# Padding so that the large on-chip tensors of a transformer kernel begin at multiples of 512 bytes

## The chip, the core and the metric

The kernel is one program on one NeuronCore of a Trainium2 chip. The engines that matter here are TensorE (PE in the profile, its weight loads PEld), VectorE (DVE), ScalarE (ACT), GpSimd (POOL) and the queue of SyncE (SP), which issues all DMAs. They share the state buffer (SBUF), in which every tensor occupies the same byte range of each of 128 partitions, and TensorE writes to eight PSUM banks. The metric is the device time of one execution in microseconds (us); lower is better. Times are compared on fresh runs of both kernels.

## The reference

One block of a conformer-like layer and two blocks of a hybrid layer over 256 tokens of width 1024, all float32. Cut to what costs time:

```python
x = x + 0.5 * swiglu_ffn(rms_norm(x), ffn1_w13, ffn1_w2)      # 1024 -> 2*2816 -> 1024
proj = rms_norm(x) @ w_in                                      # 1024 -> 2568: convolution + attention
x = x + y @ w_out
x = x + 0.5 * swiglu_ffn(rms_norm(x), ffn2_w13, ffn2_w2)
h = rms_norm(x)
h = h + gdn_mixer(rms_norm_2(h), gdn_w_in, ...)                # 1024 -> 4112, gated delta rule, -> 1024
h = h + swiglu(rms_norm_2(h), ffn_w_in[0], ffn_w_out[0])
h = h + (p[0] @ ple_w_proj[0]) * sigmoid(rms_norm_2(h) @ ple_w_gate[0])
k, v = shared_kv(h, w_kv)                                      # stick-breaking attention
h = h + sb_mixer(rms_norm_2(h), k, v, w_q, w_out)
h = h + swiglu(...); h = h + (p[1] @ ple_w_proj[1]) * sigmoid(...)
```

There are thus four feed-forward blocks, each with a product 1024 -> 5632 ("up") and one 2816 -> 1024 ("down"), three mixers and two gates.

## The kernel before

**Products.** Every large product is made from pieces of the TensorE format fp32r. A float32 number is kept as a high part and a low part, and one product of 128 rows, 128 tokens and up to 512 columns takes three matmuls (`passes`, lines 1527 to 1529):

```python
pe.matmul(psum, lhs[0], rhs[0], start=start, stop=False, ...)   # L1527
pe.matmul(psum, lhs[0], rhs[1], start=False, stop=False, ...)   # L1528
return pe.matmul(psum, lhs[1], rhs[0], start=False, stop=stop, ...)  # L1529
```

The first operand, `lhs`, is the stationary one: it is loaded into the array ahead of the matmul. The second, `rhs`, moves through the array. The profile writes `bank<-moving,stationary`, so `bank<-whi,xThi 128x512` is a matmul with 512 moving columns of the weight buffer `whi` and a stationary piece of `xThi`. Numbers in names are left out there: `xThi` also stands for `xThi2`, `xTlo` for `xTlo2`, `u` for `u4`, `y` for `y4`.

**Where the operands lie.** The weights come from memory through four ring buffers of 8192 bytes, `raw0` to `raw3` (DMA). ScalarE rounds a slot into `whi0` to `whi3` (L390), VectorE takes the rest into `wlo0` to `wlo3` (L1018). The turned activations are the other operand, one of four pairs:

- `xThi`, `xTlo`: the normalised input of the up products, the mixers, the gates and the mixers' outputs. 2976 matmuls of 128x512 have them stationary. In 864 matmuls of 128x256 (`block_cols`) they move and a piece of `whi` or `wlo` is stationary.
- `hThi`, `hTlo`: the hidden state of a feed-forward block, stationary in its down product: 22 k-tiles x 2 token tiles x 2 halves x 3 = 264 matmuls of 128x512 a block, 1056 in all.
- `xThi2`, `xTlo2`: a second normalised input, stationary in two products of the stick-breaking mixer (`block_rows(s + 4, xT2, ...)` and `s + 6`), 96 matmuls of 128x512.
- `pThi`, `pTlo`: the per-layer embedding, stationary in `ple_product`, 48 matmuls of 128x512.

The remaining matmuls are narrower: transposes by `ident`, attention scores, the delta rule. They read float32 operands that are not split.

**Allocation.** `sb(name, shape)` takes the next free bytes of every partition, rounded up to 32. `region(always, *turns)` lays several sets of tensors over the same room: the feed-forward set, the first mixer's, the second mixer's and the third mixer's all begin where the permanent tensors end. The first free byte is 1152. The permanent tensors are, in order, `raw`, `whi`, `wlo`, `X`, `xs`, `xThi`, `xTlo`, `gain`, `ident`, `ones`, `upto`, then many small tensors up to `head_gain`, then the shared room. From the declared sizes the places in a partition are, in bytes:

| tensor | start before | rest by 512 | start after | rest by 512 |
|---|---|---|---|---|
| raw0 (raw1 to wlo3 follow every 8192) | 1152 | 128 | 1536 | 0 |
| X, xs | 99456, 107648 | 128 | 99840, 108032 | 0 |
| xThi, xTlo | 115840, 124032 | 128 | 116224, 124416 | 0 |
| ident | 140416 | 128 | 140800 | 0 |
| narrow_m | 146240 | 320 | 146624 | 192 |
| shared room, hThi, qkT, vs | 149472 | 480 | 150016 | 0 |
| hTlo | 172000 | 480 | 172544 | 0 |
| xThi2, xTlo2 | 165856, 174048 | 480 | 166400, 174592 | 0 |
| pThi, pTlo | 204768, 206816 | 480 | 205312, 207360 | 0 |
| AT (delta rule) | 191584 | 96 | 190976 | 0 |
| u, y (first mixer) | 149472, 158144 | 480, 448 | 218112, 154112 | 0 |
| u4, y4 (second mixer) | 215584, 219744 | 32, 96 | 221696, 213504 | 0 |
| last byte used | 227936 | | 228480 | |

A stationary piece of the four pairs is 512 bytes a partition and begins a multiple of 512 bytes behind its tensor's start; a moving piece of `whi` or `wlo` is 2048 bytes and begins a multiple of 2048 (512 in `block_cols`, where it is stationary) behind it. So the rests of the table hold for every piece.

**Order of the work.** All five engines run instruction lists that are written out by hand, with semaphores between them. SP issues a weight slot when VectorE has finished the slot four earlier; ScalarE and VectorE split slots ahead of TensorE.

Of the kernel before, what the change touches and what calls it, by code (L numbers as in the profile page):

```python
# [6 lines left out]
F32 = mybir.dt.float32  # L7
F32R = mybir.dt.float32r
# [4 lines left out]
P = 128  # L13
# [4 lines left out]
def build_program(nc, a, out):  # L18
# [6 lines left out]
    SEQ, D = a["x"].shape[1:]  # L25
    NT = SEQ // P
# [3 lines left out]
    DC = a["conv_b"].shape[1]  # L30
    CT = DC // P
    TAPS = a["conv_w"].shape[1]
    PAD = TAPS - 1
    H1 = a["forget_b"].shape[1]
    D1 = DC // H1
    H2 = a["gdn_a_log_2"].shape[1]
    HG = H2 // 4
    W4 = a["gdn_conv_2"].shape[1]
    PAD4 = W4 - 1
# [74 lines left out]
    with ExitStack() as ctx:  # L114
        def sb(name, shape, dt=F32):
            return ctx.enter_context(nc.sbuf_tensor(name, shape, dt))
# [20 lines left out]
            return sem(engine), names.index(name) + 1  # L137

        bank = [ctx.enter_context(nc.psum_tensor(f"bank{i}", [P, 512], F32)) for i in range(8)]
        raw = [sb(f"raw{i}", [P, SLOT]) for i in range(RAW)]  # L140
        whi = [sb(f"whi{i}", [P, SLOT], F32R) for i in range(SPLIT)]
        wlo = [sb(f"wlo{i}", [P, SLOT], F32R) for i in range(SPLIT)]
# [28 lines left out]
        dt_bias = sb("dt_bias", [P, H2])  # L171
        head_gain = sb("head_gain", [P, 3, P])
        GDNG, KG, QG = range(3)

        def region(always, *turns):
            got = []
            with ExitStack() as phase:
                got += [phase.enter_context(nc.sbuf_tensor(n, s, d)) for n, s, d in always]
                for specs in turns:
                    with ExitStack() as turn:  # L180
                        got += [turn.enter_context(nc.sbuf_tensor(n, s, d)) for n, s, d in specs]
            return got
# [6 lines left out]
             ("pp", [P, NT, D], F32), ("gate_s", [P, NT, D], F32)],  # L189
            [("row_chan", [CT, P], F32), ("row_tap", [TAPS, DC], F32), ("row_tap4", [W4, QKV * P], F32)])  # L190

        (u, gs, y, a_nat, ln_row, qz, kz, v1, mask1, mask_r, ident_r, diag, zf, zfe, lf, cumx, p2, pT1, nmx, rsum, rinv, yA,
         yst, yms, yrs, y_nat, flT, c_sums, c_nmean, c_ssq, c_var, c_rstd) = region([
            ("u", [P, CT, PAD + SEQ], F32), ("gs", [P, CT, SEQ], F32), ("y", [P, CT, SEQ], F32),
            ("a_nat", [P, NT, DC], F32), ("ln_row", [P, 3, DC], F32),
            ("qz", [P, H1, SEQ], F32), ("kz", [P, H1, SEQ], F32), ("v1", [P, NT, DC], F32),
            ("mask1", [P, P], F32), ("mask_r", [P, P], F32R), ("ident_r", [P, P], F32R), ("diag", [P, CT * PE_TAPS, P], F32),
            ("zf", [P, NT, H1], F32), ("zfe", [P, NT, H1], F32),
            ("lf", [P, NT, H1], F32), ("cumx", [P, NT, H1 // 2, D1 + 1], F32),
            ("p2", [P, 2, 384], F32), ("pT1", [P, 2, 384], F32), ("nmx", [P, H1, NT], F32),  # L200
            ("rsum", [P, NT, H1], F32), ("rinv", [P, NT, H1], F32), ("yA", [P, NT, DC], F32),
            ("yst", [P, NT], F32), ("yms", [P, NT], F32), ("yrs", [P, NT], F32),
            ("y_nat", [P, NT, DC], F32), ("flT", [2 * H1, SEQ], F32), ("c_sums", [P, NT], F32), ("c_nmean", [P, NT], F32),
            ("c_ssq", [P, 2, NT], F32), ("c_var", [P, 2, NT], F32), ("c_rstd", [P, 2, NT], F32)])
        LNG, LNB, ONG = range(3)
        aff = xs[:, :, DC:]


        (qkT, sg, zab, eab, gl, lkq, vec, knat, bv, dg, dec, AT, QKT, pair, lvl, maskT, gident_r, gmask_r, S, oss, oms, ors, v_or_TU, u4, y4,
         sq4) = region(  # L210
            [("qkT", [P, 2 * H2, SEQ], F32), ("sg", [P, NT, D], F32), ("zab", [P, NT, 2 * H2], F32),
             ("eab", [P, NT, 2 * H2], F32), ("gl", [P, NT, 2 * H2], F32), ("lkq", [P, NT, 2 * H2], F32),
             ("vec", [P, 10, NT, H2], F32), ("knat", [P, H2, P], F32), ("bv", [P, NT, D], F32),
             ("dg", [P, 4, P], F32), ("dec", [P, 4, P], F32), ("AT", [P, HG, 4, P], F32),
             ("QKT", [P, HG, 4, P], F32), ("pair", [P, P], F32), ("lvl", [P, 5, 64], F32), ("maskT", [P, P], F32), ("gident_r", [P, P], F32R), ("gmask_r", [P, P], F32R), ("S", [P, H2, P], F32),
             ("oss", [P, NT, H2], F32), ("oms", [P, NT, H2], F32), ("ors", [P, NT, H2], F32),
             ("v_or_TU", [P, H2 * SEQ], F32), ("u4", [P, 4, PAD4 + SEQ], F32), ("y4", [P, 4, SEQ], F32),
             ("sq4", [P, 4, SEQ], F32)])
        abT = dg[0:4 * H2, 0:2, :].rearrange("p a b -> p (a b)")
        vT = v_or_TU[:].rearrange("p (h t) -> p h t", h=H2)  # L220

# [1960 lines left out]
```

## Time and profile before

| | |
|---|---|
| median of 3 runs | 1281.78 us (1281.6 to 1283.31) |
| the profiled execution | 1281.92 us, span of its trace 1280.2 us |
| TensorE | busy 1264.0 us of the span |
| DVE, ACT, POOL | busy 759.9, 621.4, 75.5 us |
| granted clock | 0.996 of full, on average |

"Busy" for TensorE counts a matmul from its start to a modelled end, and matmuls overlap in the array. What a matmul costs in a dense row of them is the distance from its start to the next one's start, which the timeline shows; the text calls it the step.

### The profile page before, as it was taken

To read this page: it belongs to the slowest core of one execution; us is meant where nothing else is said; L and a number is where in the kernel's file an instruction comes from. 1 tells how busy PE (TensorE), PEld (TensorE's weight loads), DVE (VectorE), ACT (ScalarE), POOL (GpSimd) and SP (SyncE) were. 2 spreads that over 40 slices of the span, in tenths; PEclk is the share of its full clock that TensorE was granted. 3 is DMA by queue.
4 is the path that set the end of the run, shared out by engine and by line. 5 is a ranking of instruction groups with operands and counts; after the bars stand their busy time and mean duration, and the time that the engine had idled before them with its cause. 6 is when DMAs were issued, how large, how long until landed. Compare 5 with 4: busy or idle time off the path is not lost.

```text
span 1280.2 us, 16498 instructions
## 1 busy us (share of the span) xinstructions
PE 1264.0 (99%) x6711; PEld 1077.9 (84%) x6711; DVE 759.9 (59%) x891; ACT 621.4 (49%) x798; POOL 75.5 (6%) x125
## 2 busy tenths in 40 slices
PE   8999999999999999999999999999999999999998
PEld 6888888988888888899999888888887888888887
DVE  4655436896654545777776655554677636545435
ACT  5544426665544433655613544443466745444433
POOL 1000002002000000400001000000023000000000
PEclk9999999999999999999998999999999999999999
DMA  8965555452566564545102476555365427665530
GB/s 271 286 182 186 192 186 151 171 172 72 172 194 190 174 227 136 194 133 188 60 1 67 122 243 194 190 177 186 135 219 174 159 59 239 190 200 180 196 132 33
DMA packets 140427, 212.27 MB, mean 166 GB/s; under 512 B 10265, under 2 KB 101277, under 8 KB 140348
## 3 DMA queue, kind: packets, MB, share of 16 engines
q1 hardware_dynamic: 140352, 211.22, 50.7%
q8 instruction: 53, 0.87, 0.3%
q14 instruction: 22, 0.18, 0.0%
HBM read 210.14 MB, written 1.05 MB: 165 GB/s over the span
## 4 chain that ended last, share of the span: by engine, by line
PE 91%; DVE 3%; ACT 3%; POOL 1%; issue 1%; DMA 1%; SPq 0%; ACTq 0%; DVEq 0%; POOLq 0%
PE bank L1527 27%; PE bank L1529 26%; PE bank L1528 26%; PE bank L1936 2%; PE bank L1666 2%; PE bank L1556 1%; PE bank L1947 1%; PE bank L1955 1%; DVE y L1126 1%; DVE wlo L1018 1%; ACT whi L390 1%; PE bank L1907 1%; PE bank L1900 1%; PE bank L1861 1%; DMA X<-in_x_dram 1%
## 5 line engine op out<-in xcount | busy, mean ns | idle before, releaser
L1018 DVE TENSOR_TENSOR wlo<-raw,whi 128x2048 fp32r<-128x2048 f32 (+1 forms) x190 | 416.4, 2196 | 289.0 <-ACT whi L390 288.8
L390 ACT ACTIVATE whi<-raw 128x2048 fp32r<-128x2048 f32 x190 | 363.1, 1915 | 237.8 <-PE bank L1529 228.6
L1527 PE MATMUL bank<-whi,xThi 128*128 128x512 f32 x1024 | 405.2, 396 | 3.1 <-DVE xTlo L1041 1.0
L1529 PE MATMUL bank<-whi,xTlo 128*128 128x512 f32 x1024 | 399.5, 390 | 0.0
L1528 PE MATMUL bank<-wlo,xThi 128*128 128x512 f32 x1024 | 398.9, 390 | 0.0
L1527 PEld LDWEIGHTS bank<-whi,xThi 128*128 128x128 f32 x1024 | 192.3, 188 | 43.2 <-issue 2.0
L1529 PEld LDWEIGHTS bank<-whi,xTlo 128*128 128x128 f32 x1024 | 192.2, 188 | 41.2
L1528 PEld LDWEIGHTS bank<-wlo,xThi 128*128 128x128 f32 x1024 | 192.5, 188 | 38.2
L1527 PE MATMUL bank<-whi,hThi 128*128 128x512 f32 x352 | 140.5, 399 | 0.0
L1529 PE MATMUL bank<-whi,hTlo 128*128 128x512 f32 x352 | 139.5, 396 | 0.0
L1528 PE MATMUL bank<-wlo,hThi 128*128 128x512 f32 x352 | 139.5, 396 | 0.0
L473 ACT ACTIVATE silu<-bank 128x256 f32<-128x256 f32 x88 | 33.6, 383 | 122.0 <-PE bank L1529 122.0
L1527 PE MATMUL bank<-xThi,whi 128*128 128x256 f32 x288 | 82.7, 287 | 0.0
L1528 PE MATMUL bank<-xTlo,whi 128*128 128x256 f32 x288 | 82.2, 286 | 0.0
L1529 PE MATMUL bank<-xThi,wlo 128*128 128x256 f32 x288 | 82.2, 285 | 0.0
L1529 PEld LDWEIGHTS bank<-whi,hTlo 128*128 128x128 f32 x352 | 66.3, 188 | 16.2
L1528 PEld LDWEIGHTS bank<-wlo,hThi 128*128 128x128 f32 x352 | 66.3, 188 | 15.6
L1527 PEld LDWEIGHTS bank<-whi,hThi 128*128 128x128 f32 x352 | 66.3, 188 | 15.6
L916 POOL TENSOR_SCALAR meansq<-sumsq 128x1 f32<-128x1 f32 x16 | 12.5, 781 | 882.8 <-ACT xs L414 699.5
L1092 DVE TENSOR_TENSOR hnat<-silu,bank 128x256 f32<-128x256 f32 x88 | 36.7, 417 | 46.7 <-ACT silu L473 46.7
L1527 PEld LDWEIGHTS bank<-xThi,whi 128*128 128x128 f32 x288 | 55.9, 194 | 0.1
L1529 PEld LDWEIGHTS bank<-xThi,wlo 128*128 128x128 f32 x288 | 56.0, 194 | 0.0
(394 smaller groups left out, 1198.3 us busy)
## 6 DMA issues: line engine op xcount, KB each, us to landing
raw<-in_ffn_w_dram SPq DMA_DIRECT2D x176, 256.0 KB, 4.1
raw<-in_ffn_w_in_dram SPq DMA_DIRECT2D x176, 256.0 KB, 3.9
raw<-in_ffn_w_dram SPq DMA_DIRECT2D x22, 1024.0 KB, 5.0
raw<-in_ffn_w_out_dram SPq DMA_DIRECT2D x22, 1024.0 KB, 5.0
raw<-in_gdn_w_in_dram SPq DMA_DIRECT2D x16, 1024.0 KB, 5.5
raw<-in_w_in_dram SPq DMA_DIRECT2D x10, 1024.0 KB, 5.1
raw<-in_ple_w_gate_dram SPq DMA_DIRECT2D x8, 1024.0 KB, 4.9
raw<-in_w_kv_dram SPq DMA_DIRECT2D x8, 1024.0 KB, 6.1
```

Source lines behind the costliest of these rows:

```text
L390: act.activation(whi[w % SPLIT][:], raw[w % RAW][:], ACT.Copy).then_inc(w_hi, 1)
L473: act.activation(silu[:, j % 2, t, :], bank[2 * (j % 2) + t][:, 0:256], ACT.Silu).then_inc(sem("ffn_silu"), 1)
L1018: dve.tensor_tensor(wlo[w % SPLIT][:, c], raw[w % RAW][:, c], whi[w % SPLIT][:, c].bitcast(F32), ALU.subtract).then_inc(w_lo, 1)
L1092: dve.tensor_tensor(hnat[:, j % 2, t, :], silu[:, j % 2, t, :], bank[2 * (j % 2) + t][:, 256:512], ALU.mult).then_inc(sem("ffn_h"), 1)
L1126: ins = dve.scalar_tensor_tensor(out=y[:, c, :], in0=src, scalar=tap[:, c, k:k + 1], in1=y[:, c, :], op0=ALU.mult, op1=ALU.add)
L1527: pe.matmul(psum, lhs[0], rhs[0], start=start, stop=False, skip_group_check=True)
L1528: pe.matmul(psum, lhs[0], rhs[1], start=False, stop=False, skip_group_check=True)
L1529: return pe.matmul(psum, lhs[1], rhs[0], start=False, stop=stop, skip_group_check=True)
L1556: ins = pe.transpose(bank[4 + b][:, k * P:(k + 1) * P], xs[:, t, (4 * b + k) * P:(4 * b + k + 1) * P], ident[:])
L1666: ins = pe.transpose(bank[4 + j % 2][:, k * SEQ + t * P:k * SEQ + (t + 1) * P], hnat[:, j % 2, t, k * P:(k + 1) * P], ident[:])
L1861: ins = pe.matmul(bank[6][:, col:col + 1], sq4[:, c, t * P:(t + 1) * P], ones[:, 0:1], start=True, stop=True)
L1936: ins = pe.matmul(bank[q][:, h * c.stop:(h + 1) * c.stop], A_[q][k, h, :], T[q][k, h, c], start=True, stop=True)
```

## The change

Two unused tensors are added, `front` (96 floats, 384 bytes) ahead of `raw0` and `level` (40 floats, 160 bytes) ahead of the shared room. The lists of the first and second mixer's tensors are put in another order: those whose size is a multiple of 512 bytes come first, the others (`u`, `cumx`, `u4`, `lvl`, `vec` and the small ones) last. Nothing else changes. On each of the five engines the built program has the same instructions in the same order with the same waits as before; only addresses differ, so no rows of the order are shown.

```diff
@@ build_program
         bank = [ctx.enter_context(nc.psum_tensor(f"bank{i}", [P, 512], F32)) for i in range(8)]
+        sb("front", [P, 96])
         raw = [sb(f"raw{i}", [P, SLOT]) for i in range(RAW)]
         whi = [sb(f"whi{i}", [P, SLOT], F32R) for i in range(SPLIT)]
...
         head_gain = sb("head_gain", [P, 3, P])
         GDNG, KG, QG = range(3)
+        sb("level", [P, 40])
 
         def region(always, *turns):
...
-            ("u", [P, CT, PAD + SEQ], F32), ("gs", [P, CT, SEQ], F32), ("y", [P, CT, SEQ], F32),
+            ("gs", [P, CT, SEQ], F32), ("y", [P, CT, SEQ], F32),
...
-            ("zf", [P, NT, H1], F32), ("zfe", [P, NT, H1], F32),
-            ("lf", [P, NT, H1], F32), ("cumx", [P, NT, H1 // 2, D1 + 1], F32),
...
+            ("y_nat", [P, NT, DC], F32), ("flT", [2 * H1, SEQ], F32),
+            ("u", [P, CT, PAD + SEQ], F32), ("cumx", [P, NT, H1 // 2, D1 + 1], F32),
...
-            [("qkT", [P, 2 * H2, SEQ], F32), ("sg", [P, NT, D], F32), ("zab", [P, NT, 2 * H2], F32),
+            [("qkT", [P, 2 * H2, SEQ], F32), ("sg", [P, NT, D], F32), ("knat", [P, H2, P], F32), ("bv", [P, NT, D], F32),
...
+             ("u4", [P, 4, PAD4 + SEQ], F32), ("lvl", [P, 5, 64], F32), ("vec", [P, 10, NT, H2], F32),
```

## Rows read from the trace of the kernel before

**Rows 1.** The page: busy time of each engine, share of the span, instructions.

```profile
span 1280.2 us, 16498 instructions
PE 1264.0 (99%) x6711; PEld 1077.9 (84%) x6711; DVE 759.9 (59%) x891; ACT 621.4 (49%) x798; POOL 75.5 (6%) x125
```

**Rows 2.** The page: the chain of work that ended last, by engine.

```profile
PE 91%; DVE 3%; ACT 3%; POOL 1%; issue 1%; DMA 1%; SPq 0%; ACTq 0%; DVEq 0%; POOLq 0%
```

**Rows 3.** Timeline of TensorE, stationary xT, up product: start us, us, instruction.

```profile
99.55 0.39 PE L1528 MATMUL bank<-wlo,xThi 128*128 128x512 f32 x1
...
104.54 0.39 PE L1529 MATMUL bank<-whi,xTlo 128*128 128x512 f32 x1
```

**Rows 4.** Timeline of TensorE, stationary hT, down product of the first block.

```profile
180.18 0.40 PE L1529 MATMUL bank<-whi,hTlo 128*128 128x512 f32 x1
180.42 0.39 PE L1527 MATMUL bank<-whi,hThi 128*128 128x512 f32 x1
...
186.74 0.40 PE L1527 MATMUL bank<-whi,hThi 128*128 128x512 f32 x1
```

**Rows 5.** Timeline of TensorE, stationary xThi2 and xTlo2, third mixer.

```profile
976.56 0.40 PE L1529 MATMUL bank<-whi,xTlo 128*128 128x512 f32 x1
...
981.48 0.40 PE L1529 MATMUL bank<-whi,xTlo 128*128 128x512 f32 x1
```

**Rows 6.** Timeline of TensorE, stationary pT, the whole first token tile.

```profile
822.37 0.39 PE L1528 MATMUL bank<-wlo,pThi 128*128 128x512 f32 x1
...
824.70 0.39 PE L1529 MATMUL bank<-whi,pTlo 128*128 128x512 f32 x1
```

**Rows 7.** Timeline of TensorE after a transpose, last gate product, stationary xT.

```profile
1262.04 0.39 PE L1528 MATMUL bank<-wlo,xThi 128*128 128x512 f32 x1
...
1263.89 0.39 PE L1527 MATMUL bank<-whi,xThi 128*128 128x512 f32 x1
...
1266.84 0.39 PE L1528 MATMUL bank<-wlo,xThi 128*128 128x512 f32 x1
```

**Rows 8.** Windows of the down product and of two windows with the lower clock.

```profile
core 0: us, PE busy (x) PEld busy (x) DVE busy (x) ACT busy (x) POOL busy (x), PEclk, DMA share, GB/s
553.00:560.00 7.00, 7.00 (x48) 7.00 (x47) 7.00 (x14) 2.69 (x3) 0.00 (x0) 0.76 0.47 151
670.00:690.00 20.00, 20.00 (x164) 19.75 (x164) 14.34 (x26) 5.96 (x24) 1.21 (x2) 0.83 0.35 106
150.00:198.00 48.00, 48.00 (x207) 38.59 (x206) 19.47 (x12) 16.03 (x12) 0.87 (x2) 1.00 0.49 165
```

**Rows 9.** Timeline of TensorE, 128x256, moving xT, stationary whi or wlo.

```profile
560.05 0.28 PE L1527 MATMUL bank<-xThi,whi 128*128 128x256 f32 x1
...
562.45 0.28 PE L1529 MATMUL bank<-xThi,wlo 128*128 128x256 f32 x1
```

**Rows 10.** Timeline of TensorE, 128x256, with 16 and 8 stationary columns.

```profile
214.91 0.28 PE L1641 MATMUL bank<-xThi,narrow_m 128*16 128x256 f32 x1
...
216.76 0.28 PE L1527 MATMUL bank<-xThi,whi 128*128 128x256 f32 x1
```

**Rows 11.** Timeline of TensorE in the delta rule: unsplit float32, merged over x8.

```profile
635.62 1.06 PE L1936 MATMUL bank<-core_hi,AT 128*128 128x128 f32 x8
636.52 1.06 PE L1936 MATMUL bank<-core_hi,xs 128*128 128x128 f32 x8
```

**Rows 12.** Groups of VectorE: the convolutions' taps.

```profile
L1126 DVE SCALAR_TENSOR_TENSOR y<-u,tap,y 128x256 f32<-128x256 f32 x96 | 39.2, 475 | 0.0
L1283 DVE SCALAR_TENSOR_TENSOR y<-u,tap,y 128x256 f32<-128x256 f32 x72 | 29.1, 480 | 0.0
```

**Rows 13.** The chain that ended last: its DMA (start us, us).

```profile
4.34 6.75 DMA X<-in_x_dram
```

**Rows 14.** The page: the DMA queue, packets, MB, share of 16 engines.

```profile
q1 hardware_dynamic: 140352, 211.22, 50.7%
```

More of the change, by code:

```diff
@@ L190, in build_program @@
             [("row_chan", [CT, P], F32), ("row_tap", [TAPS, DC], F32), ("row_tap4", [W4, QKV * P], F32)])
-        (u, gs, y, a_nat, ln_row, qz, kz, v1, mask1, mask_r, ident_r, diag, zf, zfe, lf, cumx, p2, pT1, nmx, rsum, rinv, yA,
-         yst, yms, yrs, y_nat, flT, c_sums, c_nmean, c_ssq, c_var, c_rstd) = region([
-            ("u", [P, CT, PAD + SEQ], F32), ("gs", [P, CT, SEQ], F32), ("y", [P, CT, SEQ], F32),
+        (gs, y, a_nat, ln_row, qz, kz, v1, mask1, mask_r, ident_r, diag, p2, pT1, yA, y_nat, flT, u, cumx, zf, zfe, lf,
+         nmx, rsum, rinv, yst, yms, yrs, c_sums, c_nmean, c_ssq, c_var, c_rstd) = region([
+            ("gs", [P, CT, SEQ], F32), ("y", [P, CT, SEQ], F32),
             ("a_nat", [P, NT, DC], F32), ("ln_row", [P, 3, DC], F32),
@@ L197, in build_program @@
             ("mask1", [P, P], F32), ("mask_r", [P, P], F32R), ("ident_r", [P, P], F32R), ("diag", [P, CT * PE_TAPS, P], F32),
-            ("zf", [P, NT, H1], F32), ("zfe", [P, NT, H1], F32),
-            ("lf", [P, NT, H1], F32), ("cumx", [P, NT, H1 // 2, D1 + 1], F32),
-            ("p2", [P, 2, 384], F32), ("pT1", [P, 2, 384], F32), ("nmx", [P, H1, NT], F32),
-            ("rsum", [P, NT, H1], F32), ("rinv", [P, NT, H1], F32), ("yA", [P, NT, DC], F32),
-            ("yst", [P, NT], F32), ("yms", [P, NT], F32), ("yrs", [P, NT], F32),
@@ L203, in build_program @@
-            ("y_nat", [P, NT, DC], F32), ("flT", [2 * H1, SEQ], F32), ("c_sums", [P, NT], F32), ("c_nmean", [P, NT], F32),
-            ("c_ssq", [P, 2, NT], F32), ("c_var", [P, 2, NT], F32), ("c_rstd", [P, 2, NT], F32)])
+            ("p2", [P, 2, 384], F32), ("pT1", [P, 2, 384], F32), ("yA", [P, NT, DC], F32),
+            ("y_nat", [P, NT, DC], F32), ("flT", [2 * H1, SEQ], F32),
+            ("u", [P, CT, PAD + SEQ], F32), ("cumx", [P, NT, H1 // 2, D1 + 1], F32),
+            ("zf", [P, NT, H1], F32), ("zfe", [P, NT, H1], F32), ("lf", [P, NT, H1], F32), ("nmx", [P, H1, NT], F32),
@@ L205, in build_program @@
+            ("rsum", [P, NT, H1], F32), ("rinv", [P, NT, H1], F32),
+            ("yst", [P, NT], F32), ("yms", [P, NT], F32), ("yrs", [P, NT], F32), ("c_sums", [P, NT], F32),
+            ("c_nmean", [P, NT], F32), ("c_ssq", [P, 2, NT], F32), ("c_var", [P, 2, NT], F32), ("c_rstd", [P, 2, NT], F32)])
         LNG, LNB, ONG = range(3)
         aff = xs[:, :, DC:]
-        (qkT, sg, zab, eab, gl, lkq, vec, knat, bv, dg, dec, AT, QKT, pair, lvl, maskT, gident_r, gmask_r, S, oss, oms, ors, v_or_TU, u4, y4,
-         sq4) = region(
-            [("qkT", [P, 2 * H2, SEQ], F32), ("sg", [P, NT, D], F32), ("zab", [P, NT, 2 * H2], F32),
-             ("eab", [P, NT, 2 * H2], F32), ("gl", [P, NT, 2 * H2], F32), ("lkq", [P, NT, 2 * H2], F32),
-             ("vec", [P, 10, NT, H2], F32), ("knat", [P, H2, P], F32), ("bv", [P, NT, D], F32),
-             ("dg", [P, 4, P], F32), ("dec", [P, 4, P], F32), ("AT", [P, HG, 4, P], F32),
[L215 to L218, printed above, removed]
@@ new lines, in build_program @@
+        (qkT, sg, knat, bv, dg, dec, AT, QKT, pair, maskT, gident_r, gmask_r, S, v_or_TU, y4, sq4, u4, lvl, vec,
+         zab, eab, gl, lkq, oss, oms, ors) = region(
+            [("qkT", [P, 2 * H2, SEQ], F32), ("sg", [P, NT, D], F32), ("knat", [P, H2, P], F32), ("bv", [P, NT, D], F32),
+             ("dg", [P, 4, P], F32), ("dec", [P, 4, P], F32), ("AT", [P, HG, 4, P], F32),
+             ("QKT", [P, HG, 4, P], F32), ("pair", [P, P], F32), ("maskT", [P, P], F32),
+             ("gident_r", [P, P], F32R), ("gmask_r", [P, P], F32R), ("S", [P, H2, P], F32),
+             ("v_or_TU", [P, H2 * SEQ], F32), ("y4", [P, 4, SEQ], F32), ("sq4", [P, 4, SEQ], F32),
+             ("u4", [P, 4, PAD4 + SEQ], F32), ("lvl", [P, 5, 64], F32), ("vec", [P, 10, NT, H2], F32),
+             ("zab", [P, NT, 2 * H2], F32), ("eab", [P, NT, 2 * H2], F32), ("gl", [P, NT, 2 * H2], F32),
+             ("lkq", [P, NT, 2 * H2], F32), ("oss", [P, NT, H2], F32), ("oms", [P, NT, H2], F32),
+             ("ors", [P, NT, H2], F32)])
```

## Prediction

> **What bounds the kernel now.** I read the page first: TensorE is busy for 1264.0 of 1280.2 us [rows 1], and the chain of work that ended last is 91% TensorE [rows 2]. Busy time counts overlapping matmuls, so I went on to the timeline and measured the step, from one start to the next, in stretches where no record is missing. That is the price of a matmul here, and it is what an address could change.
>
> With a piece of xT stationary, 22 steps from 99.55 to 104.54 us take 4.99 us: 226.8 ns each [rows 3]. With a piece of hT stationary, 28 steps from 180.18 to 186.74 take 6.56 us: 234.3 ns each [rows 4]. The work is the same: 128x512, moving `whi` or `wlo`, full clock (1.00 in this stretch) [rows 8]. The two stages differ in their order (a down product alternates between two banks), so the step could belong to the stage. The third mixer says otherwise: its `block_rows` runs in the up products' manner, but with `xThi2` and `xTlo2`, and 21 steps take 4.92 us: 234.3 ns [rows 5]. With pT, 10 steps take 2.33 us, 233 ns [rows 6]. And the last gate product, in the down products' manner but with xT, runs at 231.3 ns for 8 steps after a transpose and then settles: 13 steps in 2.95 us, 226.9 ns [rows 7]. So the longer step goes with the tensor that is stationary. By the table of places xT begins at rest 128 by 512, a whole number of 64 bytes; hT, xT2 and pT begin at 480, which is 32 past one.
>
> **What the change does, step by step.** No instruction, wait or queue entry is added, removed or moved; nothing is queued behind anything new.
>
> 1. Stationary pieces of hT and xT2 go from rest 480 to rest 0. I expect them to run as xT does: 234.3 - 226.8 = 7.5 ns less a step. 1056 + 96 = 1152 matmuls x 7.5 ns = 8.6 us. They lie on the path: in the stretch of the down product TensorE has no idle time in 48 us, while DVE works 19.47 us, ACT 16.03 us and the DMA engines 49% [rows 8]. A stretch shorter by 3% leaves those covers more than double what is needed, so nothing becomes late behind it.
> 2. pT: its short stretches look like the unsettled steps of xT, 233 against 231.3 ns [rows 6, 7]. 48 x 1.7 ns = 0.1 us.
> 3. xT as stationary (2976 matmuls) and the 128x256 ones (864, step 2.40 us / 20 = 120 ns [rows 9]): operands go from rest 128 to rest 0, both by the same 384 bytes, so their distance stays. No row has an fp32r operand of 128 columns at rest 0. Bounds: a gain down to the step of the nearest row with a cheaper weight load, 16 steps in 1.85 us = 115.6 ns for 16 and 8 stationary columns [rows 10], 4.4 ns less; a loss up to the 7.5 ns of hT. I take 0, because 128 is already a whole number of 64 bytes, and because the row with the smaller step has fewer columns to load as its evident reason.
> 4. Unsplit float32 matmuls: with AT stationary (rest 96, also 32 past a multiple of 64) 8 take 0.90 us, with xs (rest 128) 0.89 us [rows 11]. Price 0: these matmuls do not feel the rest.
> 5. VectorE's taps: 475 ns with one set of rests, 480 with another [rows 12]. All 168 of them at 5 ns would be 0.8 us, but DVE is 3% of the chain [rows 2]; I take 0, at most 0.2 either way.
> 6. Transfers: their engines are at 50.7% [rows 14] and only the first load, 6.75 us of X, is on the chain [rows 13]. No row shows a transfer to rest 0. I take 0; bounds 0 and a gain of 0.5 us, as a small part of that one load.
>
> Sum: 8.6 + 0.1 = 8.7 us. Against the profiled execution, 1281.92 - 8.7 = 1273.2; the median is 0.14 us lower, so 1273.1 us.
>
> A rule of the Trainium skill speaks against the whole sum. The page "SBUF — State Buffer", section "Specifications (TRN2)", gives 16-byte lines and lets a new line cost only where it has fewer than two hits. By that rule every start here, a multiple of 32 before and after, is equally good and the sum would be 0. The steps of 226.8 and 234.3 ns don't contradict the rule outright, since it could be something other than the start that tells the tensors apart; that is the first rival.
>
> **The rivals.**
>
> - *No change (0.13).* The longer step comes from where hT, xT2 and pT lie in the partition, not from the rest: all of them begin above byte 149,000, xT below 133,000, and this stays so after the change. The trace cannot part the two, since everything slow is at 480 and everything high is slow. Against it: hT, xT2 and pT are spread over 59,000 bytes and show the same step. Time 1281.8 us, or within about 1 us of it if only small terms move. The line rule of the Trainium skill's page "SBUF — State Buffer" gives this time too. The case in which the faster down product meets a late split belongs here, but the slack of rows 8 leaves it little.
> - *More than expected (0.08).* A start at 512 also frees xT and the 128x256 matmuls of some of their cost over bare streaming (512 columns at 2.4 GHz are 213.3 ns, the step 226.8). At the lower bound of step 3, 4.4 ns on all 5040 fp32r matmuls (4176 of 512 columns, 864 of 256) is 22.2 us more: 1250.9 us. Half of it gives 1262. Against it: the 120 ns of rows 9 and the 226.8 of rows 3 lie the same 13.4 ns above streaming, which looks like a fixed cost of the format. The Trainium skill's "TensorE: Matmul & The Clock Gate", section "Back-to-back issue gap", gives N/2.4 + 2.5 ns; by that page, as an estimate, the step could fall to 215.8 ns. No row of an fp32r matmul here comes down to it.
> - *Slower (0.06).* Rest 0 behaves as rest 480 does and the settled step of xT is a property of rest 128. For it: that step is not always there, it is reached only after some eight steps of 231.3 ns [rows 7], so it depends on how two streams fall against each other. Then 2976 x 7.5 ns = 22.3 us are lost and nothing is won: 1304.1 us. It decides from 2.9 ns more on the step of xT, where the 8.7 us are eaten.
>
> **How the numbers follow.** My forecast has 0.73: 1273.1, own range 1270.5 to 1276. The lower clock adds to that range: 0.76 in a 7 us window is 1.7 us lost, 0.83 in 20 us is 3.4 us [rows 8], and one such fall more or less is 1.7 us. The likeliest case and most of the no-change case (1279.5 to 1284) make up the 8 in 10, so the range reaches from 1266, which takes in a small extra gain of xT, to 1282.5. A measurement of this kernel tells about 0.2% (2.6 us) from no change. Faster than that: 0.73 + 0.08 and a little of the no-change case, 0.82. Slower: 0.06. The same: 0.12.
>
> **What the profile of the changed kernel would show.** Right: in the timeline of the first down product the step falls to 226.8 ns and so does that of `xThi2`; the first down product's 264 matmuls end 2.0 us earlier; xT and 128x256 keep 226.8 and 120. Wrong by the first rival: 234.3 in both places. Wrong by the second: under 225 in the up product. Wrong by the third: 230 or more there. It is also wrong if steps fall but the time does not; then the wait ahead of a down product's slots would show DVE or ACT as the releaser. The weakest step is the first: that the rest by 64, rather than something else that the slow tensors share, sets their step.

## The result, and the profile after

The changed kernel takes 1274.02 us (median of 6 runs, 1272.34 to 1275.8); the kernel before, on the same chip, 1281.74 us (6 runs, 1281.6 to 1283.35). The ratio is 0.9932, with a 95% interval of 0.9922 to 0.9942: 8.7 us less, between 7.4 and 10.0 (the two medians are 7.7 us apart). The prediction was 1273.1 us, with 8.7 us of gain. One execution of the kernel before, among those of the first group of experiments, had a low clock throughout (1571.78 us, 0.748 of full) and is left out of the ratios.

The profiled execution took 1272.45 us. Its page gives the span and the engines' busy times (they answer to [rows 1]), the chain by engine [rows 2] and the DMA queue [rows 14]:

```profile
span 1270.7 us, 16498 instructions
PE 1254.4 (99%) x6711; PEld 1076.0 (85%) x6711; DVE 759.9 (60%) x891; ACT 621.0 (49%) x798; POOL 75.7 (6%) x125
...
PE 91%; ACT 3%; DVE 3%; POOL 1%; issue 1%; DMA 0%; SPq 0%; ACTq 0%; DVEq 0%; POOLq 0%
...
q1 hardware_dynamic: 140352, 211.22, 50.8%
```

TensorE's busy time fell by 9.6 us and the span by 9.5; the counts, the other engines and the transfers stayed as they were. So the time came out of TensorE's matmuls, without a new wait. A step below is the distance between two printed starts divided by the number of steps; the starts are rounded to 0.01 us, so that a step worked out in this way is good to some 0.4 ns. Where it came from is in its timeline. In the down product of the first block, with hT stationary (answers to [rows 4]):

```profile
181.57 0.39 PE L1530 MATMUL bank<-whi,hThi 128*128 128x512 f32 x1
181.79 0.39 PE L1531 MATMUL bank<-wlo,hThi 128*128 128x512 f32 x1
182.02 0.39 PE L1532 MATMUL bank<-whi,hTlo 128*128 128x512 f32 x1
...
187.69 0.39 PE L1530 MATMUL bank<-whi,hThi 128*128 128x512 f32 x1
```

From the first to the last start there are 27 steps in 6.12 us: 226.7 ns, where it was 234.3. In the up product, with xT stationary (answers to [rows 3]), and in the third mixer, with xT2 (answers to [rows 5]):

```profile
109.14 0.39 PE L1531 MATMUL bank<-wlo,xThi 128*128 128x512 f32 x1
...
113.90 0.39 PE L1531 MATMUL bank<-wlo,xThi 128*128 128x512 f32 x1
...
971.52 0.39 PE L1531 MATMUL bank<-wlo,xThi 128*128 128x512 f32 x1
...
976.06 0.39 PE L1530 MATMUL bank<-whi,xThi 128*128 128x512 f32 x1
```

21 steps in 4.76 us are 226.7 ns, unchanged; 20 steps in 4.54 us are 227.0 ns (226.7 by the trace's nanoseconds), where it was 234.3. The 128x256 matmuls (answers to [rows 9]) kept their 120 ns, 19 steps in 2.28 us:

```profile
555.57 0.28 PE L1530 MATMUL bank<-xThi,whi 128*128 128x256 f32 x1
...
557.85 0.28 PE L1531 MATMUL bank<-xTlo,whi 128*128 128x256 f32 x1
```

The two spans differ by 9.5 us, the medians by 7.7. Part of that is the clock. The windows that answer to the first two of [rows 8]:

```profile
core 0: us, PE busy (x) PEld busy (x) DVE busy (x) ACT busy (x) POOL busy (x), PEclk, DMA share, GB/s
553.00:560.00 7.00, 7.00 (x60) 7.00 (x59) 5.18 (x6) 3.92 (x3) 0.00 (x0) 1.00 0.33 83
670.00:690.00 20.00, 19.51 (x158) 18.85 (x158) 14.71 (x26) 7.59 (x26) 2.20 (x2) 0.83 0.35 107
```

The fall in the first window, 7.00 x 0.24 = 1.7 us of full clock in the execution before, did not come in this one, and the two in the second did (0.17 x 20 = 3.4 us in both). By the steps it cost a little less: 16 matmuls of 256 columns took some 213 ns instead of 120, which is 1.5 us. So of the 9.5 us between the spans some 1.5 us is the clock and 8.0 us is left for the steps.

### The profile page after: what moved, and what is told of

It reads as the page before. It is cut to its first block, busy times and chain, and to the rows that moved or that the text cites. A ratio compares the mean times of both kernels' runs of the same rounds, so it can differ in the third digit from the quotient of the medians.

```text
span 1270.7 us, 16498 instructions
## 1 busy us (share of the span) xinstructions
PE 1254.4 (99%) x6711; PEld 1076.0 (85%) x6711; DVE 759.9 (60%) x891; ACT 621.0 (49%) x798; POOL 75.7 (6%) x125
## 4 chain that ended last, share of the span: by engine, by line
PE 91%; ACT 3%; DVE 3%; POOL 1%; issue 1%; DMA 0%; SPq 0%; ACTq 0%; DVEq 0%; POOLq 0%
PE bank L1530 26%; PE bank L1532 26%; PE bank L1531 26%; PE bank L1939 2%; PE bank L1669 2%; PE bank L1559 1%; PE bank L1950 1%; DVE y L1129 1%; DVE wlo L1021 1%; PE bank L1958 1%; ACT whi L393 1%; PE bank L1910 1%; PE bank L1903 1%; PE bank L1864 1%; DMA raw<-in_ffn_w_dram 0%
## 5 line engine op out<-in xcount | busy, mean ns | idle before, releaser
L1531 PEld LDWEIGHTS bank<-xTlo,whi 128*128 128x128 f32 x288 | 55.2, 192 | 0.0
```

The source lines that it names most:

```text
L1531: pe.matmul(psum, lhs[0], rhs[1], start=False, stop=False, skip_group_check=True)
```

## The experiments

Theories are named by letters in the expectations. **A**, the prediction's: the stationary piece's own start decides, by 64 bytes. **B**: the place in the partition. **C**: the distance between the starts of the stationary and the moving piece, by 64 bytes. **D**: both must begin at a multiple of 512. **E**: the distance must be 0 by 512. **F**: the distance must be 0 by 256. B had fallen with the result itself: hT and xT2 still begin above byte 149,000, and their step is 226.7 ns.

"Distance" below is the start of the stationary piece less that of the moving one, by 256 bytes. In the kernel before, xT and the weights both begin at rest 128 (distance 0), and hT, xT2 and pT at 480: 480 - 128 = 352, which is 96 by 256. The kernels of a group ran on one chip with the kernel before, whose medians there were 1283.07, 1282.99 and 1283.51 us.

### First group: the stationary piece alone, or its partner

**room_only.** The kernel before, with 32 bytes ahead of the shared room: hT and xT2 begin at rest 0, the weights stay at 128.

```diff
         GDNG, KG, QG = range(3)
+        sb("level", [P, 8])
```

> The kernel before with one unused tensor of 32 bytes ahead of the shared room, nothing else: hT, xThi2 and pT go from rest 480 to rest 0 by 512, while the weight buffers and xT stay at rest 128. Theory A (the start of the stationary piece by 64 bytes sets the step of a 512-column matmul): all of the gain, step of hT 226.8 ns, about 1273 to 1274 us. Theory B (the place in the partition, not the rest): hT keeps 234.3 ns, 1281.8 us. Theory C (the distance between moving and stationary operand by 64 bytes): the distance is again a multiple of 64, so as A. Theory D (all large tensors must begin at a multiple of 512): no or only part of the gain, above 1277 us.

Measured: 1280.2 us, ratio 0.9979 (0.997 to 0.9988). The down product:

```profile
181.60 0.40 PE L1528 MATMUL bank<-whi,hThi 128*128 128x512 f32 x1
...
187.87 0.40 PE L1528 MATMUL bank<-whi,hThi 128*128 128x512 f32 x1
```

27 steps in 6.27 us: 232.2 ns, and in the third mixer 20 steps in 4.65 us, 232.5. With exactly the rest 0 that the prediction held to be the cause, three quarters of the longer step stayed. A falls; so does C, since the distance of 128 is a multiple of 64. The small gain fits its steps: 1152 x 2 ns = 2.3 us, and 2.7 us by the ratio.

**xt_32.** The changed kernel with only xT moved to rest 32 (`back` and the smaller `level` keep all that follows).

```diff
+        sb("shift", [P, 8])
         with ExitStack() as lent:
...
         xTlo = sb("xTlo", [P, KD, SEQ], F32R)
+        sb("back", [P, 8])
...
-        sb("level", [P, 40])
+        sb("level", [P, 24])
```

> The changed kernel with xThi and xTlo (and what shares their room) 32 bytes further, at rest 32 by 64; weights and the shared room stay at rest 0. A: the 2976 matmuls with xT stationary take 234.3 instead of 226.8 ns, 22.3 us more than the changed kernel, about 1296 us; the 864 matmuls of 256 columns, where xT moves, keep 120 ns. B: xT is low in the partition and keeps 226.8 ns, about 1274 us. C: as A for the 512-column ones, and the 256-column ones get slower too, by up to 7.5 ns each, 6.5 us more, about 1302 us.

Measured: 1287.02 us, ratio 1.0037 (1.0023 to 1.0051), slower than the kernel before. The up product, and the 128x256 matmuls of the second mixer:

```profile
101.59 0.40 PE L1533 MATMUL bank<-wlo,xThi 128*128 128x512 f32 x1
...
106.49 0.40 PE L1533 MATMUL bank<-wlo,xThi 128*128 128x512 f32 x1
...
560.49 0.28 PE L1532 MATMUL bank<-xThi,whi 128*128 128x256 f32 x1
...
562.70 0.28 PE L1533 MATMUL bank<-xTlo,whi 128*128 128x256 f32 x1
```

21 steps in 4.90 us: 233.3 ns with xT, while hT stayed at 227.0. The 128x256 matmuls went the other way, 19 steps in 2.21 us, 116.3 ns (116.8 as the mean of all settled ones). That was in no expectation. The sum in this run: over all steps whose records stand side by side, xT went from a mean of 227.4 to 233.0 ns, 2976 x 5.6 = 16.7 us where 22.3 was expected, and those of 256 columns from 120.6 to 117.6, 864 x 3.0 = 2.6 us back; 14.1 us net, and its span is 13.7 us longer than the changed kernel's, with the clock falling equally often in both.

**weights_32.** The changed kernel with the weight buffers at 32, xT at 64 and hT at 0: distances 32 and -32.

```diff
+        sb("shift", [P, 8])
         whi = [sb(f"whi{i}", [P, SLOT], F32R) for i in range(SPLIT)]
...
+        sb("back", [P, 8])
...
-        sb("level", [P, 40])
+        sb("level", [P, 24])
```

> The changed kernel with whi and wlo at rest 32 by 64, everything else at a multiple of 64. A: the 512-column matmuls, where the weights move, keep 226.8 ns; the 864 of 256 columns, where they are stationary, take up to 7.5 ns more, at most 6.5 us: 1274 to 1280 us. B: no change, about 1274 us. C: every product's distance is off by 32, so all 4176 matmuls of 512 columns take 234.3 ns: 31 us more, and up to 6.5 us for the narrow ones, 1305 to 1312 us.

Measured: 1294.28 us, ratio 1.0087 (1.0071 to 1.0103). xT and hT in the up and the down product:

```profile
101.88 0.40 PE L1533 MATMUL bank<-wlo,xThi 128*128 128x512 f32 x1
...
106.78 0.40 PE L1533 MATMUL bank<-wlo,xThi 128*128 128x512 f32 x1
...
181.72 0.40 PE L1533 MATMUL bank<-wlo,hThi 128*128 128x512 f32 x1
...
188.03 0.39 PE L1533 MATMUL bank<-wlo,hThi 128*128 128x512 f32 x1
```

233.3 and 233.7 ns (both 233.3 over all their settled steps). hT is at a multiple of 512 and xT at one of 64, and both have the longer step: the partner counts. The sign of a distance of 32 makes no difference.

**xt_and_weights_32.** Weights and xT both at 32, hT at 0: the same as weights_32 but that `back` stands behind `xTlo`.

```diff
+        sb("shift", [P, 8])
         whi = [sb(f"whi{i}", [P, SLOT], F32R) for i in range(SPLIT)]
...
         xTlo = sb("xTlo", [P, KD, SEQ], F32R)
+        sb("back", [P, 8])
...
-        sb("level", [P, 40])
+        sb("level", [P, 24])
```

> The changed kernel with both whi, wlo and xThi, xTlo at rest 32 by 64; the shared room stays at rest 0. A: xT slow as stationary (22.3 us) and the weights slow as stationary (up to 6.5 us): 1296 to 1303 us; hT stays at 226.8 ns. C: the distance of xT to the weights is a multiple of 64 again, so xT is fast, and hT, xThi2 and pT are off by 32 and slow: 1282 to 1283 us, as the kernel before. B: about 1274 us.

Measured: 1280.43 us, ratio 0.9983 (0.9974 to 0.9993).

```profile
101.60 0.39 PE L1533 MATMUL bank<-wlo,xThi 128*128 128x512 f32 x1
...
106.36 0.39 PE L1533 MATMUL bank<-wlo,xThi 128*128 128x512 f32 x1
...
181.62 0.40 PE L1532 MATMUL bank<-whi,hThi 128*128 128x512 f32 x1
...
187.93 0.39 PE L1532 MATMUL bank<-whi,hThi 128*128 128x512 f32 x1
```

xT at rest 32 runs at 226.7 ns here and ran at 233.3 in xt_32: the same start, another partner. hT at rest 0 has 233.7 ns (233.3 over all its settled steps). What is left is a rule of the two starts together.

### Second group: by how many bytes the distance counts

**all_128.** The kernel before with 160 bytes ahead of the shared room, and nothing else: weights, xT, hT, xT2 and pT all at rest 128; no `front`, no other order of the lists.

```diff
         GDNG, KG, QG = range(3)
+        sb("level", [P, 40])
```

> The kernel before with 160 unused bytes ahead of the shared room and nothing else: weights, xT, hT, xThi2 and pT all at rest 128 by 512. Theory E (formed after the first four runs: a 512-column matmul takes 226.8 ns only where the stationary piece and the moving piece begin at the same rest by 512; the rest itself is free): all of the gain, hT at 226.8 ns, 1272 to 1275 us. Theory D (the rest must be 0 by 512): hT stays above 232 ns, 1280 us as in the run with 32 bytes. Theory A (stationary rest by 64 alone) has already fallen for that run and would give the full gain too.

Measured: 1274.24 us (1272.58 to 1276.26), ratio 0.9932 (0.992 to 0.9945).

```profile
181.23 0.39 PE L1529 MATMUL bank<-wlo,hThi 128*128 128x512 f32 x1
...
187.57 0.39 PE L1530 MATMUL bank<-whi,hTlo 128*128 128x512 f32 x1
```

28 steps in 6.34 us: 226.4 ns, and 226.7 by the trace's nanoseconds. This one line has the whole gain of the change. D falls: nothing large begins at a multiple of 512.

**all_32.** The changed kernel with 32 bytes more in front: every large tensor at rest 32.

```diff
-        sb("front", [P, 96])
+        sb("front", [P, 104])
```

> [...] E: no change, 1272 to 1275 us, steps of 226.8 ns everywhere. A: all 4176 wide matmuls at 233 ns or more, 26 to 31 us more, above 1300 us. D: slower than the changed kernel, by an amount it does not say.

Measured: 1277.39 us, ratio 0.9956 (0.9943 to 0.997). The steps are the short ones, 27 in 6.12 us with hT, 226.7 ns:

```profile
181.52 0.39 PE L1531 MATMUL bank<-wlo,hThi 128*128 128x512 f32 x1
...
187.64 0.39 PE L1531 MATMUL bank<-wlo,hThi 128*128 128x512 f32 x1
```

So a stationary piece that is 32 past a multiple of 64 costs nothing, the plainest case against the prediction's step. The time is 3.4 us longer than the changed kernel's all the same. Two windows show part of why:

```profile
50.00:57.00 7.00, 7.00 (x25) 5.58 (x25) 2.89 (x2) 0.49 (x2) 0.00 (x0) 0.76 0.85 254
553.00:560.00 7.00, 7.00 (x48) 7.00 (x47) 6.49 (x12) 2.51 (x4) 0.00 (x0) 0.76 0.40 142
```

The granted clock fell in both, and in neither of them in the changed kernel; with the two between 670 and 690 us, which both executions have, this one had four falls against two. The profiled spans are 1275.6 and 1270.7 us. Of these 4.9 us the two additional falls are some 3.3 us: the steps with xT add up to 1.8 us more and those of the 256-column matmuls to 1.5. The other 1.6 us I can't place. Executions of the two kernels with the same mean clock of 0.994 differ by about as much, 1275.6 to 1276.0 against 1274.0 us of span, though on two chips.

**h256_x64.** The changed kernel with hT at 256 and xT2 at 64, weights at 0.

```diff
-            [("hThi", [P, KF, SEQ], F32R), ("hTlo", [P, KF, SEQ], F32R),
+            [("shift", [P, 64], F32), ("hThi", [P, KF, SEQ], F32R), ("hTlo", [P, KF, SEQ], F32R),
...
-            ("vs", [P, NT, D], F32), ("kn", [P, NT, D], F32), ("xThi2", [P, KD, SEQ], F32R), ("xTlo2", [P, KD, SEQ], F32R),
+            ("vs", [P, NT, D], F32), ("kn", [P, NT, D], F32), ("shift2", [P, 16], F32), ("xThi2", [P, KD, SEQ], F32R), ("xTlo2", [P, KD, SEQ], F32R),
```

> The changed kernel with hT and pT at rest 256 and xThi2, xTlo2 at rest 64; weights and xT at rest 0. It asks with which period the distance counts. E (512): hT above 231 ns, xT2 above 231 ns, 1280 to 1283 us. F (256): hT at 226.8 ns, 1273 to 1275 us, xT2 above 231 ns. C (64): both at 226.8 ns, 1272 to 1275 us, although the run with 32 bytes ahead of the room speaks against it.

Measured: 1275.78 us, ratio 0.9943 (0.993 to 0.9957). hT, and xT2:

```profile
181.62 0.39 PE L1530 MATMUL bank<-whi,hThi 128*128 128x512 f32 x1
...
187.74 0.39 PE L1530 MATMUL bank<-whi,hThi 128*128 128x512 f32 x1
...
974.97 0.39 PE L1531 MATMUL bank<-wlo,xThi 128*128 128x512 f32 x1
...
979.64 0.39 PE L1530 MATMUL bank<-whi,xThi 128*128 128x512 f32 x1
```

A distance of 256 is as good as none, 226.7 ns: E falls. A distance of 64 costs, 20 steps in 4.67 us, 233.5 ns (233.3 over all its settled steps): C falls again, and the longer step is nothing of odd 32-byte starts. F is left.

**h16_x384.** hT at 16 (its tensors made 16 bytes longer, the product reading from the fifth element on), xT2 at 384, with the changed kernel's other places.

```diff
-            [("hThi", [P, KF, SEQ], F32R), ("hTlo", [P, KF, SEQ], F32R),
+            [("hThi_", [P, 4 + KF * SEQ], F32R), ("even1", [P, 120], F32), ("hTlo_", [P, 4 + KF * SEQ], F32R), ("even2", [P, 120], F32),
...
+        hThi, hTlo = (x[:, 4:].rearrange("p (k t) -> p k t", k=KF) for x in (hThi_, hTlo_))
...
+            ("vs", [P, NT, D], F32), ("kn", [P, NT, D], F32), ("shift2", [P, 96], F32), ("xThi2", [P, KD, SEQ], F32R), ("xTlo2", [P, KD, SEQ], F32R),
```

> The changed kernel with hT at rest 16 and xThi2, xTlo2 at rest 384; pT, weights and xT at rest 0. E: a distance of 16 bytes is a distance, so hT goes above 231 ns and the time to 1280 to 1283 us; xT2 above 231 ns. If only distances of a whole SBUF line of 32 or 64 bytes count: hT keeps 226.8 ns and the time stays at 1273 to 1275 us.

The expectation's "line of 32 or 64 bytes" is a supposition; no run shows a line of either size. Measured: 1277.98 us, ratio 0.996 (0.9946 to 0.9973). xT2: 232.5 ns, as room_only's distance of 128, which 384 is by 256. hT gave something new. The same product in the first block, and in the third:

```profile
181.24 0.39 PE L1533 MATMUL bank<-whi,hTlo_ 128*128 128x512 f32 x1
...
187.59 0.39 PE L1531 MATMUL bank<-whi,hThi_ 128*128 128x512 f32 x1
...
869.70 0.39 PE L1532 MATMUL bank<-wlo,hThi_ 128*128 128x512 f32 x1
...
875.77 0.40 PE L1531 MATMUL bank<-whi,hThi_ 128*128 128x512 f32 x1
```

28 steps in 6.35 us are 226.8 ns; 26 steps in 6.07 us are 233.5. Transposes cut each of the four down products into three rows of hT matmuls: 24, 228 and 12. In the first, second and fourth product the 24 ran long (233.4 ns), the 228 short (226.7) and the 12 long; in the third the 24 and the 228 ran long (855 to 908 us) and the 12 short. Each of the twelve rows keeps one pace to its end. Its first step, from its first matmul to its second, was 312 or 313 ns ahead of the four short rows and 314 to 319 ns ahead of the eight long ones. So at a distance of 16 both paces are possible, and a row keeps the one it has fallen into.

### Third group: the other distances, one operand of two, and a version for both widths

The first three were one execution each, so their times have no interval; their steps are what counts.

**h128_x192** and **h96_x160** are h256_x64 with other sizes of `shift` and `shift2`: 32 and 48 floats, 24 and 40 floats.

> The changed kernel with hT and pT at rest 128 and xThi2, xTlo2 at rest 192; weights and xT at rest 0. Theory F (the distance of the two operands counts by 256): hT as at distance 384, 232.3 to 232.5 ns; xT2 at 192 above 230 ns. One look, about 1280 us. If the sign of the distance mattered and the period were 512, hT could have any step from 226.7 to 235.

> The changed kernel with hT and pT at rest 96 and xThi2, xTlo2 at rest 160; weights and xT at rest 0. F: 96 is the same as the 352 of the kernel before by 256, so hT shows 234.3 ns, and about 1282 us; xT2 at 160 above 230 ns. Period 512 would leave hT free to differ from 234.3.

Measured: 1279.98 us, hT 27 steps in 6.27 us, 232.2 ns, xT2 21 steps in 4.81 us, 229.0 ns, less than the 230 that was expected at least; and 1282.95 us. The rows are those of xT2 in h128_x192 and of hT in h96_x160:

```profile
977.33 0.39 PE L1530 MATMUL bank<-whi,xThi 128*128 128x512 f32 x1
...
982.14 0.39 PE L1530 MATMUL bank<-whi,xThi 128*128 128x512 f32 x1
...
181.51 0.39 PE L1530 MATMUL bank<-whi,hThi 128*128 128x512 f32 x1
...
188.07 0.39 PE L1531 MATMUL bank<-wlo,hThi 128*128 128x512 f32 x1
```

28 steps in 6.56 us, 234.3 ns for hT in h96_x160, and 233.5 ns for its xT2. h96_x160 has the distance of the kernel before, 96, at other addresses, and its step comes back to the tenth of a nanosecond. h128_x192 repeats the 232.2 of room_only.

**hi32_lo0.** Only hThi is at 32, hTlo stays at 0.

```diff
+            [("shift", [P, 8], F32), ("hThi", [P, KF, SEQ], F32R), ("back", [P, 56], F32), ("hTlo", [P, KF, SEQ], F32R),
...
```

> The changed kernel with hThi 32 bytes on, at rest 32, and hTlo at rest 0 by 256; all else at rest 0. In a down product two of three matmuls then have a stationary piece at distance 32. If each matmul pays for itself (F, simplest form): 2 x 233.3 + 226.7 over 3, 231.1 ns on average, the longer ones on the first two of the three lines, if the loading of the next piece pays, on the first and third. If only a row of matmuls that all have distance 0 can settle: 233 ns on all three. One look, 1277 to 1280 us.

Measured: 1277.65 us; 27 steps in 6.26 us, 231.9 ns. If each matmul paid by its own distance, two of three steps would be long, (2 x 233.3 + 226.7) / 3 = 231.1. The mean is near that, but the three kinds of step are 231.9, 230.9 and 233.2 ns, and none of them is 226.7; nor are all three 233, as they would be if only a row with distance 0 throughout could settle. The steps from the first and the third of the three lines are longer than that from the second, which is the order of the form in which the next piece's load pays, but not its sizes. Whether a matmul pays for its own pair, or for the next stationary piece that is loaded beside it, this does not settle.

**mixer_32.** The changed kernel, with xT written and read 32 bytes later in the second mixer alone, where the 128x256 matmuls are (rooms 64 floats longer, second views from element 8).

```diff
...
+        xThis, xTlos = (x[:, 8:8 + KD * SEQ].rearrange("p (k t) -> p k t", k=KD) for x in xT_room)
...
-                block_rows(s, xT, [bank[0], bank[1]], k_ready=tile_ready("n4"), tilewise=True)
+                block_rows(s, xTs, [bank[0], bank[1]], k_ready=tile_ready("n4"), tilewise=True)
...
-                    block_cols(s + 2 * b, xT, [bank[2 * (b % 2)], bank[2 * (b % 2) + 1]], halfway=None if b else gate_logits)
+                    block_cols(s + 2 * b, xTs, [bank[2 * (b % 2)], bank[2 * (b % 2) + 1]], halfway=None if b else gate_logits)
```

> The changed kernel, with the input of the second mixer alone written 32 bytes further on in its buffers (64 spare floats behind each of xThi and xTlo). There 576 matmuls of 256 columns move it, which took 116.8 ns at distance 32 against 120.0 at distance 0, and 96 of 512 columns have it stationary, which took 233.3 against 226.7. F with these steps: 576 x 3.2 = 1.8 us won, 96 x 6.6 = 0.6 us lost, 1.2 us less than the changed kernel, ratio to the kernel before 0.992; too little to be told in the time, but to be seen in the steps. If distance has no such opposite effect on 256 columns: 0.6 us more than the changed kernel.

Measured: 1274.38 us (1272.61 to 1276.14), ratio 0.9926 (0.9912 to 0.9939).

```profile
555.58 0.28 PE L1535 MATMUL bank<-xThi,wlo 128*128 128x256 f32 x1
...
557.80 0.28 PE L1533 MATMUL bank<-xThi,whi 128*128 128x256 f32 x1
```

19 steps in 2.22 us, 116.8 ns (116.7 by the trace's nanoseconds) instead of 120.0. The steps say 576 x 3.2 - 96 x 6.6 = 1.2 us less (the 96 matmuls of 512 columns that read the moved xT get the longer step). The intervals of 0.9926 and 0.9932 overlap, so as a time this is no better than the changed kernel; it is seen in the steps only.

### What the groups say together

The settled step of a 512-column fp32r matmul with 128 stationary columns, at full clock, by distance. The numbers here are means over all settled steps of the trace in its nanoseconds, from the thirteenth step after a break on, so they can be 0.4 ns beside those of the short stretches above:

| distance by 256 | step, ns | seen in |
|---|---|---|
| 0 | 226.7 | changed kernel; all_128; all_32; h256_x64 (hT, 256); xT before |
| 16 | 226.7 or 233.3 | h16_x384 (hT) |
| 32 | 233.3 | xt_32, weights_32 (xT) |
| 64 | 233.3 | h256_x64 (xT2) |
| 96 | 234.3 | before (hT, xT2); h96_x160 (hT) |
| 128 | 232.3 to 232.5 | room_only; h128_x192 (hT); h16_x384 (xT2, 384) |
| 160 | 233.4 | h96_x160 (xT2) |
| 192 | 228.9 | h128_x192 (xT2, both of its products) |
| 224 | 233.3 | weights_32, xt_and_weights_32 (hT) |

## Why the prediction was right

**Step 1, the size: right. The cause it named: wrong.** The prediction held that pieces of hT and xT2 "go from rest 480 to rest 0" and are freed by that, and that "the rest by 64" sets the step. It is shown not to: rest 0 has 232.2 ns in room_only and 233.7 in xt_and_weights_32, rest 32 has 226.7 in all_32. What counts is the distance to the moving weights, by 256 bytes. In the kernel before, xT happened to have the weights' rest, so the two explanations gave the same steps; the sum needed only that hT comes to xT's step, and was right by that. That the time came out was luck in this one respect: the change happened to put the weights at the same rest as hT. The argument looked at the stationary operand's row in the table of places and not at the other one. Had it been asked for the effect of 32 bytes ahead of the room, this step would have said 8.6 us, and 2.7 came.

The size: over all steps with their records side by side, hT's mean went from 234.2 to 227.1 ns, 1056 x 7.1 = 7.5 us; with 96 x 7.5 = 0.7 of xT2 that is 8.2, against the 8.6 of the settled steps. The difference is in the first ten or so steps after transposes, which have a mean of 229 to 231 ns after the change and so gain less. The rest of the 9.5 us between the spans is the clock, 1.5 us, which the prediction allowed for in its range at 1.7 us a fall.

**Step 2, pT: right.** Its 40 steps inside a row went from 233.1 to 230.2 ns, 48 x 2.9 = 0.1 us.

**Step 3, nothing for xT and the 128x256 matmuls: right,** for the reason it gave in passing: both operands moved by the same 384 bytes, "so their distance stays". Its upper bounds were too wide in one direction and it missed that the narrow matmuls could be changed by a distance at all.

**Steps 4 to 6: 0, as taken.** VectorE's taps are 480 and 479 ns now (they answer to [rows 12]): the first set went up by 5 ns, the second down by 1.

```profile
L1129 DVE SCALAR_TENSOR_TENSOR y<-u,tap,y 128x256 f32<-128x256 f32 x96 | 39.3, 480 | 0.0
L1286 DVE SCALAR_TENSOR_TENSOR y<-u,tap,y 128x256 f32<-128x256 f32 x72 | 29.1, 479 | 0.0
```

The chain's one DMA is now a load of weights (it answers to [rows 13]). It lies in the chain for 5.64 us from 2.39 and ends at 8.03, where X ended at 11.09. DMA is 0% of the chain instead of 1%. Up to the first matmul with hT the two executions are 0.3 us apart (139.8 and 139.5 us), so at most that was gained at the start, within the bound of 0.5.

```profile
2.39 5.64 DMA raw<-in_ffn_w_dram
...
197.37 0.87 PE bank L1559 x8
```

The same group in the chain of the kernel before:

```profile
199.55 0.87 PE bank L1556 x8
```

**What it said the profile would show.** The x8 rows are transposes that stand behind 252 of the first down product's 264 matmuls. From that product's first matmul to them it takes 197.37 - 139.5 = 57.9 us instead of 199.55 - 139.8 = 59.8: 1.9 us shorter, as 252 x 7.5 ns is; 2.0 was said for all 264. The steps of xThi2, xT and the 128x256 matmuls came as written.

**The rivals.** "No change" fell with the first timeline of the changed kernel, since hT lies as high as before. The line rule of the Trainium skill's page "SBUF — State Buffer", section "Specifications (TRN2)", gives this time as well: by it all starts here, multiples of 16, are equally good. The traces disagree, 226.7 against 233.3 ns for 32 bytes of xT's start; what it says of one access may hold, but it does not tell how two streams run together. "More than expected": no settled stretch at full clock went under 226.7 ns a step at any of the places tried. "Slower" was wrong in its form, since rest 0 was as good as rest 128. But the remark in it, that the step "depends on how two streams fall against each other", was nearer to the cause than step 1 was; it should have been a theory of its own, with a distance in it.

**What stays open.** Why the distance counts, and by 256, is not shown: the trace has no record inside a matmul. The table is no smooth curve: most distances have 233.3 ns, but 96, 128, 192 and 16 behave in their own ways, and hi32_lo0 did not tell whose load is in whose way. I didn't try to move the moving operand by itself for one matmul of a pair, nor the output bank.

## What to carry to other kernels

For back-to-back fp32r matmuls of 512 columns, look at the starts of both SBUF operands and make their difference a multiple of 256 bytes (0 and 256 were tried); where they begin by themselves did not matter at rests 0, 32 and 128 by 512. If matmuls of 256 columns with the same operands take more of the time, measure first: there 32 bytes of distance were better than none. One pad of 160 bytes ahead of the later tensors did what the reordering to multiples of 512 did. Before naming the property of a tensor that costs time, list that of its partner too: a pad that moves one of the two is the run that tells them apart.

## What was not expected of the hardware

- 128x256 matmuls go the other way: 120.0 ns at distance 0, and 116.3 to 116.8 ns with the stationary weights 32 bytes short of the moving xT (xt_32, mixer_32). Of these two distances each width has its own better one; no run gave the narrow matmuls a third.
- Two stable paces at a distance of 16 bytes, 226.7 and 233.3 ns, for a whole row of 228 matmuls in some 52 us. The row's first step told them apart, 312 against 316 ns. Together with the steps of 231.3 ns after transposes [rows 7] it suggests that the pace of a row of matmuls depends on how the row began, not only on its shapes; no run varied the beginning alone.
- At full clock no step comes down to streaming: 512 columns at 2.4 GHz are 213.3 ns, and the shortest settled step anywhere here is 226.7. The Trainium skill's page "TensorE: Matmul & The Clock Gate", section "Back-to-back issue gap", gives 2.5 ns over streaming; for fp32r with 128 stationary columns no run here shows less than 13 at 512 columns, or than 9 at 256 (106.7 ns of streaming against 116.3).
- At the lower clock the steps do come down to it, and a distance of 32 costs nothing. These are 512-column matmuls of weights_32, at distance 32, and 256-column ones of the kernel before, at distance 0, both with a granted clock of 1.2 GHz:

```profile
51.50 0.63 PE L1532 MATMUL bank<-whi,xThi 128*128 128x512 f32 x1
...
54.49 0.58 PE L1533 MATMUL bank<-wlo,xThi 128*128 128x512 f32 x1
...
553.47 0.41 PE L1529 MATMUL bank<-xThi,wlo 128*128 128x256 f32 x1
...
556.67 0.32 PE L1529 MATMUL bank<-xThi,wlo 128*128 128x256 f32 x1
```

7 steps in 2.99 us are 427 ns and 15 in 3.20 us are 213.3; 512 and 256 columns at 1.2 GHz are 426.7 and 213.3. The other distance gives the same: 426.4 ns in all_32 (0) and 213.3 in mixer_32 (32).

- The granted clock falls for some us to its lower level, 1.2 GHz, at a cost of 1.5 to 1.8 us each: three falls in the execution before, two in the one after, four in all_32. TensorE was busy for the whole of the window from 553 us in all three executions, whether the clock fell in it or not. Executions of one kernel differ by this as well: the changed kernel's six spans run from 1270.6 us at a mean clock of 0.997 to 1274.0 at 0.994. A difference of 3 us between two executions can be mostly this.
